# Cross attention over the memory on one Trainium2 core: probabilities divided by GpSimd before their transposes, attention output written already transposed, weight low parts moved to VectorE

## The chip, the cores and the metric

The kernel runs on 1 core of a Trainium2 chip. The metric is the device time of one execution in microseconds (us); the kernel before takes 676.6 us (median of 3 runs, 676.42 to 676.83). TensorE is the matmul engine (PE), VectorE is DVE, ScalarE is ACT, GpSimd is POOL.

## The reference

One layer of a hybrid model over 512 tokens of width 1024: a state-space mixer and block attention, then attention over a memory of 256 rows, then a convolutional feed-forward layer. The change lies in the second of these:

```
def memory_cross_attention(h, mem_n, w_q, w_kv, w_o, qn, kn):
    q = rms_norm((h @ w_q).reshape(bsz, t, X_HEADS, X_HEAD_DIM), qn)
    kv = mem_n @ w_kv
    k = rms_norm(kv[..., :D_X].reshape(bsz, m, X_HEADS, X_HEAD_DIM), kn)
    v = kv[..., D_X:].reshape(bsz, m, X_HEADS, X_HEAD_DIM)
    s = jnp.einsum('bqhd,bmhd->bhqm', q, k).astype(jnp.float32) * (X_HEAD_DIM ** -0.5)
    prob = jax.nn.softmax(s, axis=-1).astype(v.dtype)
    o = jnp.einsum('bhqm,bmhd->bqhd', prob, v).reshape(bsz, t, D_X)
    return o @ w_o
```

with 4 heads of width 128 (X_HEADS, X_HEAD_DIM), 512 query tokens t and 256 memory rows m. All is float32.

## The kernel before, in words

Tokens are cut into 4 tiles of 128. Each engine has a program of its own, an order written out by hand, and engines meet at semaphores alone. The large products are made of three matmuls each (`mm3`, L517): a float32 operand is split into a high part (made by ACT, `split_hi` L489 for weights, `tile_hi` L1203 for activations) and a low part (the remainder; DVE, `split_lo` L505 and `tile_lo` L1692), and high x high, high x low and low x high are added up in one PSUM bank. Eight PSUM banks are handed out by a table written at L282 to L344: `fill` waits until the bank's former user was drained, `filled` tells the reader, `drained` frees it.

Attention over the memory is a pipeline over 16 heads s = 0..15 (tile t = s // 4, head h = s % 4), L2486 on PE, L1336 on ACT, L1859 on DVE. For each head, in iteration s unless another is given:

- PE, scores (L2462), two heads ahead: 128 queries x 256 memory rows, into bank 3, 4 or 5.
- DVE, the negated row maximum (`row_max` L1852), one head ahead.
- ACT, one head ahead (`x_probabilities` L1322): maximum times the query's norm factor, then exp into one of two slots of `pbuf`, with the row sum into `lsum`. It waits until PE has transposed head s-2 out of that slot.
- PE, two 128x128 transposes of the unnormalised probabilities into bank 6 (`prob_transposes` L2276).
- Evacuation into `ptb` (`xp_evac` L405): ACT for even heads, DVE for odd ones.
- PE, one head later, values (`x_values` L2308): stationary operand is the transposed probabilities, moving operand is V, so queries lie on partitions; four heads fill bank 7.

After the fourth head of a tile, DVE's `normalise` (L1683) multiplies the bank by the reciprocals of the four row sums into `yrow`; PE transposes that tile by four 128x128 transposes (`xo_transposes` L2469), ACT makes the high and DVE the low part (`xo_hi` L1316, `xo_lo` L1826), and PE multiplies by w_o in four pieces (`xo_piece` L2422; each 6 matmuls of 512 columns). Between the heads PE runs other work: pieces of the query projection (`xq_piece`) up to s = 6, then those of the output projection, (0,0) at s = 7 up to (2,0) at s = 15; (2,1) to (3,3) follow after the loop. The weights of w_o are units U_XO + 0..3. Their high parts are made by ACT at s = 5..8 (`XO_AT`), their low parts by POOL (`output_low` L972), which has little else to do here: norm factors (`pow_event` L876). `w_residual` (L1830, DVE) adds a finished half tile to `hres` and frees its bank. `root` (L1438, DVE) sharpens POOL's factor by four small operations, `qx_event` (L1823, DVE) sums the squares of a query tile, `transposed` (L1642, DVE) brings a transposed query tile in.

In DVE's loop every iteration begins with the row maximum; then come, where due, the normalisation, the evacuation of head s-1, the query tile, `qx_event`, `root`, `xo_lo` and `w_residual`.

Of the kernel before, what the change touches and what calls it, by code (L numbers as in the profile page):

```python
# [20 lines left out]
TT = T // 128  # L21
# [6 lines left out]
M = 256  # L28
MT = M // 128
# [76 lines left out]
def layer(nc, A, out):  # L106
# [11 lines left out]
    with ctx:  # L118
# [149 lines left out]
        logit_ready, pv_done = sem("logit_ready"), sem("pv_done")  # L268
        rl_ready, rlrow_ready, ya_ready = sem("rl_ready"), sem("rlrow_ready"), sem("ya_ready")
        yasq_ready, yasum_ready = sem("yasq_ready"), sem("yasum_ready")  # L270
        qr_ready = sem("qr_ready")
        conv_ready, gate_ready = sem("conv_ready"), sem("gate_ready")
        hff_ready, res_ready = sem("hff_ready"), sem("res_ready")
        cube_sq, cube_ready, cube_tanh, half_ready = (sem(n) for n in ("cube_sq", "cube_ready", "cube_tanh", "half_ready"))


        QXT_BANK, XO_BANK, W_BANK = (0, 1, 2, 0), (1, 0, 1, 7), (2, 1, 2, 0, 2, 1, 3, 2)


        uses, fills = {}, [0] * 8  # L280
# [5 lines left out]
        def plan():  # L286
            use(4, "nmix"); use(5, "lam")
            for b in range(4):
                use(b, f"xa{b}")
            for b in range(4):  # L290
                use(4 + b, f"xc{b}")
            use(6, "cr"); use(7, "cm"); use(4, "xb"); use(5, "par"); use(6, "relb")
            for m in range(4):
                use(m, f"u{m}")

            def four(pre):
                for i in range(4):
                    use(6 + i % 2, f"{pre}{i}")
            for p in "qkv":
                for t in range(TT):  # L300
                    use(t, f"{p}{t}")
            for q in range(NQ):
                use(4, f"w1r{q}"); use(5, f"w1i{q}"); use(6, f"ka{q}"); use(7, f"kb{q}")
                use(4, f"vr{q}"); use(5, f"vi{q}")
                if q > 0:
                    four(("qt", "m", "kt")[q - 1])
                use(6, f"ye{q}"); use(7, f"yo{q}")
            for s in range(TT * H):
                use(3 + s % 2, f"sc{s}"); use(5 + s % 2, f"pt{s}")
                if s >= H and s % H == 0:  # L310
                    use(5, f"rl{s // H - 1}")
            for t in range(TT):
                use(7, f"pv{t}")
            use(5, "rl3"); use(6, "sa")
            use(0, "mk0"); use(1, "mk1"); use(2, "mv0"); use(0, "mv1")
            use(1, "z0"); use(2, "z1"); use(0, "z2"); use(1, "z3")
            use(3, "kx0"); use(4, "kx1")
            for t in range(TT):
                for half in range(2):
                    use((2 * t + half) % 3, f"g{t}{half}")  # L320
            for t in range(TT):
                for half in range(2):
                    use((2 * t + half + 2) % 4, f"o{t}{half}")
                    use(4 + (2 * t + half) % 4, f"x2{t}{half}")
            for t in range(TT):
                use(t % 3, f"qx{t}"); use(QXT_BANK[t], f"qxt{t}")

            for s in range(TT * XH):
                use(3 + s % 3, f"xs{s}"); use(6, f"xp{s}")
            for t in range(TT):  # L330
                use(7, f"xpv{t}"); use(XO_BANK[t], f"xo{t}")
                for half in range(2):
                    use(W_BANK[2 * t + half], f"w{t}{half}")
            for t in range(TT):
                for half in range(2):
                    use(4 + (2 * t + half) % 4, f"x3{t}{half}")
            for j in range(2 * FT):
                use(j % 4, f"f{j}")
            for x in range(4):
                for t in range(2):  # L340
                    use(E_BANK[x][t], f"e{x}{t}")
            for x in range(3):
                for t in range(2):
                    use(E_BANK[x][t], f"d{x}{t}")  # L344
# [448 lines left out]
        def _(pool):  # L793
# [175 lines left out]
                link(add(yasq[:, 2, :], yasq[:, 2, :], yasq[:, 3, :]))  # L969
                add(yasum[:, t, :], yasum[:, t, :], yasq[:, 2, :]).then_inc(yasum_ready, 1)  # L970

            def output_low(i):  # L972

                u = U_XO + i
                pool.wait_ge(hi_done, u + 1)
                nc.gpsimd.tensor_tensor(w_unit(u, 1), raw_unit(u), w_unit(u, 0).bitcast(f32), ALU.subtract)\
                    .then_inc(lo_done, 1)

            factor_rows(0)
            link(y_sum(1))  # L980
# [7 lines left out]
            attention_sum(2)  # L988
            factor_rows(3)
            attention_sum(3)  # L990
            for i in range(EVN["ya"], len(EV)):
                pow_event(i)
                if EV[i][0] == "qx2":
                    pool.wait_ge(lo_done, U_XO)
                    for n in range(4):
                        output_low(n)

            def hidden_sums(i):

# [13 lines left out]
        def _(act):  # L1013
# [300 lines left out]
                drained(A_(sqr_x[:, t % 2, :], p[:, :], ACT.Square, scale=rs[:, c:c + 1]), f"qx{t}")  # L1314

            def xo_hi(t):  # L1316
                tile_hi(f"xo{t}", bs[:, 0, :].rearrange("p (a n) -> p a n", a=4)[:, :, t * 128:(t + 1) * 128])

            qx_rows(0)
            qx_rows(1)  # L1320
# [88 lines left out]
        def _(dve):  # L1409
# [270 lines left out]
            dve.wait_ge(far_zero, 1)  # L1680
            dve.wait_ge(bias_in, 16)

            def normalise(bank, l0, heads, width, t):  # L1683

                p = read(dve, bank)
                link(V.reciprocal(rl[:, 0:heads], lsum[:, l0:l0 + heads]))
                drained(tt(yrow[:, t, :].rearrange("p (h n) -> p h n", h=heads),
                           p[:, :].rearrange("p (h n) -> p h n", h=heads),
                           rl[:, 0:heads].unsqueeze(2).to_broadcast([128, heads, width]), ALU.mult), bank)
                after_drain(dve, bank)  # L1690

            def tile_lo(name, hi, lo, last=True):  # L1692

                ins = lo_of(read(dve, name)[:, :].rearrange("p (a n) -> p a n", a=4), hi, lo)
# [130 lines left out]

            def xo_lo(t):  # L1826
                v = [bs[:, i, :].rearrange("p (a n) -> p a n", a=4)[:, :, t * 128:(t + 1) * 128] for i in range(2)]
                tile_lo(f"xo{t}", v[0], v[1])

            def w_residual(t, halves=range(2)):  # L1830
                for half in halves:
# [20 lines left out]
            def row_max(s):  # L1852
# [2 lines left out]
                V.tensor_reduce(nmx[:, 32 + s:33 + s], p[:, 0:M], AX.X, ALU.max, negate=True)\  # L1855
                    .then_inc(logit_ready, 1)

            row_max(0)
            for s in range(TT * XH):  # L1859
                if s + 1 < TT * XH:  # L1860
                    row_max(s + 1)
                if s in (5, 9, 13):
                    t = (s - 5) // 4
                    normalise(f"xpv{t}", 32 + XH * t, XH, XD, t)
                if s >= 2 and s % 2 == 0:
                    xp_evac(dve, V.tensor_copy, s - 1)
                if s in (1, 5, 9):
                    transposed("qxt", qT, "x_qn", XD ** -0.5, [1 + s // 4])
                if s in (4, 8):
                    qx_event(1 + s // 4)  # L1870
                if s in (2, 6, 10):
                    root(f"qx{1 + s // 4}", qr_ready)
                if s in (6, 10, 14):
                    xo_lo((s - 6) // 4)
                if s in (10, 12):
                    w_residual(0, [s // 2 - 5])
                if s == 14:
                    w_residual(1, [0])
                    x3_mean(0)
            xp_evac(dve, V.tensor_copy, TT * XH - 1)  # L1880
            normalise(f"xpv{TT - 1}", 32 + XH * (TT - 1), XH, XD, TT - 1)
            x3_rows(0)
            w_residual(1, [1])
            xo_lo(TT - 1)
            w_residual(2, [0])
            x3_mean(1)
            w_residual(2, [1])
# [110 lines left out]
        def _(pe):  # L1998
# [275 lines left out]
                            filled(last, f"sc{s + b}")  # L2274

            def prob_transposes(pre, sc, s, tiles, ring, last_of_fill=True):  # L2276
                after_drain(pe, f"{sc}{s}")
                p = fill(pe, f"{pre}{s}")
                for a in range(tiles):
                    last = tr(p[:, a * 128:(a + 1) * 128], pbuf[:, s % ring, a * 128:(a + 1) * 128])  # L2280
                if last_of_fill:
                    filled(last, f"{pre}{s}")
# [25 lines left out]
            def x_values(s):  # L2308
                t, h = s // XH, s % XH
                after_drain(pe, f"xp{s}")  # L2310
                p = fill(pe, f"xpv{t}") if h == 0 else pb[uses[f"xpv{t}"][0]]
                for a in range(MT):
                    last = mm(p[:, h * XD:(h + 1) * XD], ptb[:, s % 2, a * 128:(a + 1) * 128],
                              xv[:, a, h * XD:(h + 1) * XD], a == 0, a == MT - 1)
                if h == XH - 1:
                    filled(last, f"xpv{t}")
                else:
                    last.then_inc(pv_done, 1)
# [147 lines left out]
                p = fill(pe, f"xs{s}")  # L2466
                filled(mm(p[:, 0:M], qT[:, h, t * 128:(t + 1) * 128], kxT[:, h, :]), f"xs{s}")

            def xo_transposes(t):  # L2469
                after_drain(pe, f"xpv{t}")  # L2470
                tile_transposes(f"xo{t}", yrow[:, t, :])

            def x3_transposes(t):
                pe.wait_ge(xn_ready, NMK + t + 1)
                h_transposes("x3", t, x3row[:, t % 2, :])
# [10 lines left out]
            for s in range(TT * XH):  # L2486
# [7 lines left out]
                    xq_piece((s + 1) // XH + 2, (s + 1) % XH)  # L2494
                else:
                    if (s + 1) % XH == 0:
                        after_drain(pe, f"xo{(s + 1) // XH - 2}")
                    xo_piece((s + 1) // XH - 2, (s + 1) % XH)
                prob_transposes("xp", "xs", s, MT, 2)
                if s >= 1:  # L2500
                    x_values(s - 1)
                if s in (5, 9, 13):
                    xo_transposes((s - 5) // 4)
            x_values(TT * XH - 1)
            for i in range(1, 4):
                xo_piece(2, i)
                if i == 2:
                    xo_transposes(3)
            x3_transposes(0)
            after_drain(pe, "xo3")  # L2510
            for i in range(4):
                xo_piece(3, i)
                if i == 1:
# [82 lines left out]
```

## Time and profile before

| | |
|---|---|
| median of 3 runs | 676.6 us (676.42 to 676.83) |
| the profiled execution | 676.84 us |
| its span in the profile | 675.0 us |
| PE busy | 664.4 us, 98% |
| DVE busy | 489.7 us, 73% |
| ACT busy | 345.0 us, 51% |
| POOL busy | 178.6 us, 26% |
| loop over the 16 heads | about 269 to 311 us of the span |
| granted TensorE clock | 1.00 in this stretch |

The profiled execution takes 1.8 us more than its span, which lies around it and does not depend on the kernel's middle. In a timeline a row is start, duration, engine, line of the code, operation, output and inputs, and in brackets the idle time of the engine ahead of it with what ended it. Matmuls overlap, so what one costs PE is the distance from its start to the start of the next; on DVE and ACT one instruction starts some 0.08 to 0.1 us before the record of the one ahead ends. A float32 matmul is two instructions, a transpose one.

### The profile page before, as it was taken

Reading aid. Unit: us, or ns where it says so; the run is one execution under the profiler, and the core shown is the slowest. Engines: PE = TensorE matmul, PEld = TensorE weight load, DVE = VectorE, ACT = ScalarE, POOL = GpSimd, SP = SyncE. Lnnn points to the kernel's source line nnn. Section 1 sums busy time; section 2 is a strip of 40 time slices with the busy share of each in tenths; the row PEclk is TensorE's granted clock in tenths of the full one; section 3 lists DMA queues with packets and bytes.
Section 4 is the critical chain, followed back from the end, with each engine's and each line's share of the span. In section 5 each row is a group of like instructions: output and inputs, shape, how many; then the busy total and the mean of one; then the engine's idle time right before and its main releaser. Section 6 shows DMA issues by size and latency. Waiting matters only on the chain.

```text
span 675.0 us, 10889 instructions
## 1 busy us (share of the span) xinstructions
PE 664.4 (98%) x4039; PEld 550.3 (82%) x4039; DVE 489.7 (73%) x807; ACT 345.0 (51%) x602; POOL 178.6 (26%) x184
## 2 busy tenths in 40 slices
PE   7999999999999999999999999999999999999997
PEld 6978877877778788888998888888888888888886
DVE  3999998849765657556877675666566687867967
ACT  4747654676844544664454433333333454554662
POOL 4899997033221101240101111011101121100000
PEclk9999999999999999999999999999999999999999
DMA  8737563577210215030337557555556446654563
GB/s 257 225 82 183 118 186 102 156 223 258 64 63 2 98 59 187 1 124 1 126 125 249 191 186 242 191 183 187 190 191 227 146 183 210 226 186 141 178 197 124
DMA packets 73919, 105.76 MB, mean 157 GB/s; under 512 B 21929, under 2 KB 48852, under 8 KB 72340
## 3 DMA queue, kind: packets, MB, share of 16 engines
q1 hardware_dynamic: 70612, 98.89, 45.3%
q10 hardware_dynamic: 3264, 6.31, 2.9%
q8 instruction: 25, 0.41, 0.2%
q14 instruction: 18, 0.15, 0.1%
HBM read 88.27 MB, written 17.31 MB: 156 GB/s over the span
## 4 chain that ended last, share of the span: by engine, by line
PE 82%; DMA 4%; POOL 4%; ACT 4%; SPq 3%; DVE 2%; issue 1%; DVEq 0%; ACTq 0%; POOLq 0%
PE pb L519 24%; PE pb L521 24%; PE pb L520 23%; PE pb L2000 7%; PE pb L2003 4%; POOL F L802 2%; ACT F L1022 2%; SPq L679 2%; DMA raw<-in_w_in 1%; DMA F<-F 1%; DMA raw<-in_x_wkv 1%; DVE F L1420 1%; DMA F<-scr_y 1%; SPq L692 0%; ACT xs L1022 0%
## 5 line engine op out<-in xcount | busy, mean ns | idle before, releaser
L519 PE MATMUL pb<-xs,wring 128*128 128x512 f32 (+1 forms) x448 | 165.3, 369 | 0.1
L521 PE MATMUL pb<-xs,wring 128*128 128x512 f32 (+1 forms) x448 | 164.2, 366 | 0.0
L520 PE MATMUL pb<-xs,wring 128*128 128x512 f32 (+1 forms) x448 | 164.1, 366 | 0.0
L1426 DVE SCALAR_TENSOR_TENSOR F<-pb,ccol,F 128x511 f32<-128x511 f32 x88 | 65.9, 749 | 71.7 <-ACT F L1022 69.9
L509 DVE TENSOR_TENSOR wring<-raw,wring 128x1024 fp32r<-128x1024 f32 x73 | 97.5, 1338 | 6.1 <-ACT wring L498 5.9
L519 PE MATMUL pb<-wring,xs 128*128 128x512 f32 x240 | 99.1, 413 | 0.5 <-DVE wring L512 0.3
L519 PEld LDWEIGHTS pb<-xs,wring 128*128 128x128 f32 x448 | 84.5, 189 | 14.5 <-issue 0.6
L521 PEld LDWEIGHTS pb<-xs,wring 128*128 128x128 f32 x448 | 84.5, 189 | 13.7
L520 PEld LDWEIGHTS pb<-xs,wring 128*128 128x128 f32 x448 | 84.5, 189 | 13.5
L521 PE MATMUL pb<-wring,xs 128*128 128x512 f32 x240 | 94.0, 392 | 0.0
L520 PE MATMUL pb<-wring,xs 128*128 128x512 f32 x240 | 93.7, 390 | 0.0
L1022 ACT ACTIVATE F<-pb,ccol 128x512 f32<-128x512 f32 x44 | 34.3, 779 | 115.3 <-PE pb L521 115.1
L498 ACT ACTIVATE wring<-raw 128x1024 fp32r<-128x1024 f32 x78 | 81.8, 1054 | 15.1 <-DMA raw<-in_w_in 6.5
L519 PE MATMUL pb<-wring,bs 128*128 128x512 f32 x170 | 68.6, 404 | 0.6 <-DVE wring L1420 0.5
L828 POOL TENSOR_TENSOR F<-F 128x256 f32<-128x256 f32 x27 | 21.8, 809 | 172.8 <-DVE F L1420 171.4
L521 PE MATMUL pb<-wring,bs 128*128 128x512 f32 x170 | 66.3, 390 | 0.0
L520 PE MATMUL pb<-wring,bs 128*128 128x512 f32 x170 | 66.2, 390 | 0.0
L1022 ACT ACTIVATE F<-pb 16x128 f32<-16x128 f32 (+5 forms) x84 | 31.1, 383 | 56.9 <-PE pb L2003 49.0
L2000 PE MATMUL pb<-F 128*64 128x64 f32 (+6 forms) x1056 | 58.5, 256 | 1.5 <-DVE F L1420 0.7
L2000 PEld LDWEIGHTS pb<-F 128*64 128x64 f32 (+4 forms) x1056 | 45.2, 143 | 14.0 <-issue 10.6
L519 PEld LDWEIGHTS pb<-wring,xs 128*128 128x128 f32 x240 | 45.1, 188 | 12.0 <-issue 1.6
L521 PEld LDWEIGHTS pb<-wring,xs 128*128 128x128 f32 x240 | 45.1, 188 | 10.0
(160 smaller groups left out, 989.6 us busy)
## 6 DMA issues: line engine op xcount, KB each, us to landing
raw<-in_ffn_w_up SPq DMA_DIRECT2D x22, 1024.0 KB, 5.2
F<-in_ffn_w_down SPq DMA_DIRECT2D x11, 1024.0 KB, 5.0
scr_w<-F SPq DMA_DIRECT2D x11, 1024.0 KB, 3.9
F<-in_x SPq DMA_DIRECT2D x8, 512.0 KB, 5.9
raw<-in_w_in ACTq DMA_DIRECT2D x4, 1024.0 KB, 6.0
raw<-in_w_out SPq DMA_DIRECT2D x4, 1024.0 KB, 4.9
raw<-scr_w SPq DMA_DIRECT2D x8, 512.0 KB, 3.8
raw<-scr_w SPq DMA_DIRECT2D x15, 256.0 KB, 4.7
```

The costliest lines, as they stand in the source:

```text
L498: ins = nc.scalar.activation(w_unit(u, 0), raw_unit(u), ACT.Copy)
L509: ins = nc.vector.tensor_tensor(w_unit(u, 1), raw_unit(u), w_unit(u, 0).bitcast(f32), ALU.subtract)
L519: nc.tensor.matmul(ps, lh, rh, start=first, stop=False)
L520: nc.tensor.matmul(ps, lh, rl_, start=False, stop=False)
L521: return nc.tensor.matmul(ps, ll, rh, start=False, stop=last)
L679: sync.dma_start(toep[d * CG:(d + 1) * CG, :, (L - 1 - d) * CG:], kt[0:CG, :, 0:(d + 1) * CG]).then_inc(t_in[q], 16)
L802: return nc.gpsimd.tensor_tensor(o, a, b, ALU.mult)
L828: return nc.gpsimd.tensor_tensor(o, a, b, ALU.subtract)
L1022: return nc.scalar.activation(o, i, f, **k)
L1426: return V.scalar_tensor_tensor(out=o, in0=a, scalar=s1, in1=b, op0=o1, op1=o2)
L2000: return nc.tensor.matmul(o, l, r, start=start, stop=stop)
L2003: return nc.tensor.transpose(o, i, ident[0:i.shape[0], 0:i.shape[0]])
```

## The change

- The 16 row sums get a reciprocal each on DVE (`inverse_sum`), behind DVE's other work of iteration s-1, and POOL multiplies the 128x256 probabilities of each head in place (`scale_probabilities`). PE's transposes of head s wait for that in place of ACT's exp.
- `x_values` swaps its operands: V is stationary, the transposed probabilities move, so the output has head dimensions on partitions. `normalise` and `xo_transposes` are gone, and `xo_hi` and `xo_lo` read the bank of the values.
- The row maximum is taken two heads ahead on DVE.
- The low parts of the four units of w_o are made on DVE at s = 6..9, in place of POOL.
- PSUM banks are handed out anew, and the last `xo_lo` stands ahead of `w_residual(1, [1])`.

```diff
-        QXT_BANK, XO_BANK, W_BANK = (0, 1, 2, 0), (1, 0, 1, 7), (2, 1, 2, 0, 2, 1, 3, 2)
+        QXT_BANK, XPV_BANK, W_BANK = (0, 1, 2, 7), (7, 1, 7, 1), (2, 0, 2, 0, 2, 3, 0, 2)
...
-            def output_low(i):
-
-                u = U_XO + i
-                pool.wait_ge(hi_done, u + 1)
-                nc.gpsimd.tensor_tensor(w_unit(u, 1), raw_unit(u), w_unit(u, 0).bitcast(f32), ALU.subtract)\
-                    .then_inc(lo_done, 1)
+            def scale_probabilities(s):
+
+                pool.wait_ge(xinv_ready, s + 1)
+                nc.gpsimd.tensor_scalar_mul(pbuf[:, s % 2, 0:M], pbuf[:, s % 2, 0:M], rl[:, s % 4:s % 4 + 1])\
+                    .then_inc(xprob_ready, 1)
...
-            for i in range(EVN["ya"], len(EV)):
+            for i in range(EVN["ya"], EVN["qx2"]):
                 pow_event(i)
-                if EV[i][0] == "qx2":
-                    pool.wait_ge(lo_done, U_XO)
-                    for n in range(4):
-                        output_low(n)
+            for s in range(TT * XH):
+                if s in (6, 10):
+                    pow_event(EVN["qx2"] + s // 10)
+                scale_probabilities(s)
+            for i in range(EVN["x30"], len(EV)):
+                pow_event(i)
...
+            def inverse_sum(s):
+
+                after_drain(dve, f"xs{s}")
+                V.reciprocal(rl[:, s % 4:s % 4 + 1], lsum[:, 32 + s:33 + s]).then_inc(xinv_ready, 1)
+
             row_max(0)
+            row_max(1)
+            inverse_sum(0)
             for s in range(TT * XH):
-                if s + 1 < TT * XH:
-                    row_max(s + 1)
-                if s in (5, 9, 13):
-                    t = (s - 5) // 4
-                    normalise(f"xpv{t}", 32 + XH * t, XH, XD, t)
+                if s + 2 < TT * XH:
+                    row_max(s + 2)
...
                 if s in (6, 10, 14):
                     xo_lo((s - 6) // 4)
+                if s + 1 < TT * XH:
+                    inverse_sum(s + 1)
+                if s - 1 in XO_AT:
+                    split_lo(dve, U_XO + XO_AT.index(s - 1))
                 if s in (10, 12):
                     w_residual(0, [s // 2 - 5])
...
             xp_evac(dve, V.tensor_copy, TT * XH - 1)
-            normalise(f"xpv{TT - 1}", 32 + XH * (TT - 1), XH, XD, TT - 1)
             x3_rows(0)
+            xo_lo(TT - 1)
             w_residual(1, [1])
-            xo_lo(TT - 1)
...
             def prob_transposes(pre, sc, s, tiles, ring, last_of_fill=True):
-                after_drain(pe, f"{sc}{s}")
+                if pre == "xp":
+                    pe.wait_ge(xprob_ready, s + 1)
+                else:
+                    after_drain(pe, f"{sc}{s}")
...
                 for a in range(MT):
-                    last = mm(p[:, h * XD:(h + 1) * XD], ptb[:, s % 2, a * 128:(a + 1) * 128],
-                              xv[:, a, h * XD:(h + 1) * XD], a == 0, a == MT - 1)
+                    last = mm(p[:, h * XD:(h + 1) * XD], xv[:, a, h * XD:(h + 1) * XD],
+                              ptb[:, s % 2, a * 128:(a + 1) * 128], a == 0, a == MT - 1)
...
                 if s >= 1:
                     x_values(s - 1)
-                if s in (5, 9, 13):
-                    xo_transposes((s - 5) // 4)
             x_values(TT * XH - 1)
             for i in range(1, 4):
                 xo_piece(2, i)
-                if i == 2:
-                    xo_transposes(3)
             x3_transposes(0)
-            after_drain(pe, "xo3")
+            after_drain(pe, "xpv3")
```

## Rows read from the trace of the kernel before

**Rows 1.** The page, busy time by engine: busy us, share, instructions
```profile
PE 664.4 (98%) x4039; PEld 550.3 (82%) x4039; DVE 489.7 (73%) x807; ACT 345.0 (51%) x602; POOL 178.6 (26%) x184
```

**Rows 2.** Engines in a window of the span: us, busy (count) by engine, clock, DMA
```profile
262.00:325.00 63.00, 62.73 (x351) 52.81 (x351) 38.09 (x92) 35.88 (x85) 15.12 (x11) 1.00 0.16 57
```

**Rows 3.** Timeline of PE, the start of the loop and iterations 5 to 8
```profile
270.89 0.38 PE L2003 MATMUL pb<-ident,pbuf 128*128 128x128 f32 x2
...
284.43 0.60 PE L2003 MATMUL pb<-ident,F 128*128 128x128 f32 x4
284.86 0.60 PE L2000 MATMUL pb<-F 128*128 128x256 f32 x2
...
287.60 0.58 PE L519 MATMUL pb<-wring,bs 128*128 128x512 f32 x1
...
292.76 0.60 PE L2000 MATMUL pb<-F 128*128 128x256 f32 x2
293.30 0.50 PE L519 MATMUL pb<-wring,bs 128*128 128x512 f32 x1
```

**Rows 4.** Timeline of PE, iterations 10 to 15
```profile
297.93 1.04 PE L2000 MATMUL pb<-F 128*128 128x128 f32 x6
298.69 0.51 PE L519 MATMUL pb<-wring,bs 128*128 128x512 f32 x1
...
305.85 0.60 PE L2003 MATMUL pb<-ident,F 128*128 128x128 f32 x4
306.20 0.47 PE L519 MATMUL pb<-wring,bs 128*128 128x512 f32 x1
...
307.88 0.61 PE L2000 MATMUL pb<-F 128*128 128x128 f32 x4
308.62 0.47 PE L519 MATMUL pb<-wring,bs 128*128 128x512 f32 x1
```

**Rows 5.** Timeline of DVE: reciprocal, evacuation, squares, row maximum
```profile
281.69 0.18 DVE L1686 RECIPROCAL rl<-lsum 128x4 f32<-128x4 f32 x1 [1.32 <-PE pb L2000]
...
289.65 0.42 DVE L412 COPY F<-pb 128x256 f32<-128x256 f32 x1 [1.24 <-PE pb L2003]
290.00 0.68 DVE L1468 TENSOR_REDUCE sq<-F 128x4 f32<-128x512 f32 x1
...
290.78 0.42 DVE L1855 TENSOR_REDUCE nmx<-pb 128x1 f32<-128x256 f32 x1
```

**Rows 6.** Timeline of DVE: root, low part of the output, residual, a weight's low part
```profile
296.58 0.16 DVE L1420 TENSOR_TENSOR rt<-rs 128x4 f32<-128x4 f32 x1 [0.88 <-POOL rs L879]
...
297.26 0.69 DVE L1426 SCALAR_TENSOR_TENSOR bs<-pb,bs 128x512 fp32r<-128x512 f32 x1
297.87 0.68 DVE L1426 SCALAR_TENSOR_TENSOR F<-pb,F 128x512 f32<-128x512 f32 x1
...
320.88 1.22 DVE L509 TENSOR_TENSOR wring<-raw,wring 128x1024 fp32r<-128x1024 f32 x1
```

**Rows 7.** Timeline of ACT: end of the first head's exp
```profile
270.47 0.19 ACT L1022 ACTIVATION_READ_ACCUMULATOR pbuf<-pb,nmx,rs 128x1 f32 x1
```

**Rows 8.** Groups of POOL's instructions by form: count, busy us, mean ns
```profile
L976 POOL TENSOR_TENSOR wring<-raw,wring 128x1024 fp32r<-128x1024 f32 x4 | 9.5, 2380 | 5.0 <-ACT wring L498 5.0
...
L958 POOL COPY F<-rl 128x512 f32<-128x512 f32 x4 | 2.5, 621 | 18.6 <-DVE rl L1711 18.6
...
L828 POOL TENSOR_TENSOR pbuf<-F,pbuf 128x256 f32<-128x256 f32 x2 | 2.1, 1038 | 0.2
...
L831 POOL TENSOR_SCALAR sp<-sp 128x16 f32<-128x16 f32 x3 | 0.6, 205 | 0.3
```

**Rows 9.** Timeline: POOL and DVE at the same time in the stage before
```profile
157.44 1.55 POOL L952 TENSOR_SCALAR F<-F 128x512 f32<-128x512 f32 x1
157.54 1.63 DVE L509 TENSOR_TENSOR wring<-raw,wring 128x1024 fp32r<-128x1024 f32 x1
```

**Rows 10.** Timeline of POOL and of DVE, a small operation beside POOL's low part
```profile
283.66 2.37 POOL L976 TENSOR_TENSOR wring<-raw,wring 128x1024 fp32r<-128x1024 f32 x1 [2.52 <-ACT wring L498]
...
284.59 1.46 DVE L1420 TENSOR_TENSOR rt<-rs 128x4 f32<-128x4 f32 x1
```

More of the change, by code:

```diff
@@ L270, in layer @@
         yasq_ready, yasum_ready = sem("yasq_ready"), sem("yasum_ready")
-        qr_ready = sem("qr_ready")
+        qr_ready, xinv_ready, xprob_ready = sem("qr_ready"), sem("xinv_ready"), sem("xprob_ready")
         conv_ready, gate_ready = sem("conv_ready"), sem("gate_ready")
@@ L325, in plan @@
             for t in range(TT):
-                use(t % 3, f"qx{t}"); use(QXT_BANK[t], f"qxt{t}")
+                use(t % 3, f"qx{t}")
+                if t < TT - 1:
+                    use(QXT_BANK[t], f"qxt{t}")
             for s in range(TT * XH):
@@ L330, in plan @@
             for t in range(TT):
-                use(7, f"xpv{t}"); use(XO_BANK[t], f"xo{t}")
+                if t == 2:
+                    use(QXT_BANK[3], "qxt3")
+                use(XPV_BANK[t], f"xpv{t}")
                 for half in range(2):
@@ L1316, in xo_hi @@
             def xo_hi(t):
-                tile_hi(f"xo{t}", bs[:, 0, :].rearrange("p (a n) -> p a n", a=4)[:, :, t * 128:(t + 1) * 128])
+                tile_hi(f"xpv{t}", bs[:, 0, :].rearrange("p (a n) -> p a n", a=4)[:, :, t * 128:(t + 1) * 128])
             qx_rows(0)
@@ L1681, in _ @@
             dve.wait_ge(bias_in, 16)
[L1683 to L1690, printed above, removed]
             def tile_lo(name, hi, lo, last=True):
@@ L1827, in xo_lo @@
                 v = [bs[:, i, :].rearrange("p (a n) -> p a n", a=4)[:, :, t * 128:(t + 1) * 128] for i in range(2)]
-                tile_lo(f"xo{t}", v[0], v[1])
+                tile_lo(f"xpv{t}", v[0], v[1])
             def w_residual(t, halves=range(2)):
@@ L2467, in x_scores @@
                 filled(mm(p[:, 0:M], qT[:, h, t * 128:(t + 1) * 128], kxT[:, h, :]), f"xs{s}")
-            def xo_transposes(t):
-                after_drain(pe, f"xpv{t}")
-                tile_transposes(f"xo{t}", yrow[:, t, :])
             def x3_transposes(t):
@@ L2496, in _ @@
                     if (s + 1) % XH == 0:
-                        after_drain(pe, f"xo{(s + 1) // XH - 2}")
+                        after_drain(pe, f"xpv{(s + 1) // XH - 2}")
                     xo_piece((s + 1) // XH - 2, (s + 1) % XH)
```

## The prediction

> **What bounds the kernel now.** I began with the page's busy times [rows 1]: PE is busy for 664.4 of 675.0 us. Then I took the stretch that the change touches out of the table of windows [rows 2]: PE is busy for 62.73 of 63 us at full granted clock, DVE for 38, ACT for 36 and POOL for 15. So work taken off DVE, ACT or POOL buys nothing by itself. Only two things move the end: PE instructions that vanish, and waits of PE that vanish or appear. The third view, the timeline of PE [rows 3, 4], shows which waits there are, and the fourth, DVE's timeline [rows 5, 6], how late DVE is in each iteration. Averages mislead here: DVE is busy 60% of the stretch, yet its in-order queue decides when PE may start a piece.
>
> **What PE loses.** The four groups of four output transposes go. From the start of such a group to the next instruction it is 284.86 - 284.43 = 0.43 us in front of scores [rows 3] and 306.20 - 305.85 = 0.35 us in front of a piece [rows 4]. Two are of either kind: 0.43 + 0.43 + 0.35 + 0.35 = 1.56 us. The swap of operands in the values keeps count and shape (two float32 products of 128 columns by 128x128 per head): 0, since weight loads run beside matmuls for both; no row shows the swapped form, and I bound it at 0.05 us a head either way. `normalise` leaves DVE; PE never waited on it visibly.
>
> **What is added on the path to a transpose.** exp, then reciprocal on DVE, then the multiplication on POOL, then the transposes. The reciprocal has 0.18 us [rows 5]. No row shows a scaling of 128x256 on POOL. Nearest from below: a one-input copy of 128x512 takes 0.62 and a 128x16 scaling 0.205 [rows 8], which gives a line of 0.84 ns a column and 0.40 us for 256 columns; half the copy, 0.31, is the lower end. From above, a two-input operation on the same buffer and size takes 1.04 [rows 8]. I take 0.40, as the operation has one input like the copy. Each hand-over between engines costs about 0.05 to 0.1.
>
> At the first head nothing covers this. Its exp ends at 270.47 + 0.19 = 270.66 [rows 7], and PE transposes at 270.89 [rows 3]. Now: 270.66 + 0.05 + 0.18 + 0.13 + 0.40 + 0.08 = 271.50, so **+0.6 us**. For all later heads exp starts once PE has transposed the head two before, that is two iterations ahead: an iteration without query transposes is 2.74 - 0.25 = 2.49 us, so 4.98. ACT is busy for 36 us over 16 heads in the stretch [rows 2], 2.2 us a head with everything that could stand ahead of an exp, and the 0.8 us above follow: 3.0 of 4.98, so **0**. That cover is gone only if POOL needs over 2 us a head.
>
> **What DVE makes late.** This is the main term. With the maximum two heads ahead, DVE's iteration s begins with scores s+2, and these are PE's first work of iteration s itself. Everything due in that DVE iteration stands behind them. Measured from the start of those scores: filled at 0.60 [rows 3], hand-over 0.05, maximum 0.34 (0.42 less the 0.08 by which the next record overlaps), evacuation 0.35, `qx_event` 0.78 [rows 5], `root` 0.68, `xo_lo` 0.61, residual or weight low part to its end 0.68 or 1.22 [rows 6], reciprocal 0.10 of spacing, hand-over to PE 0.04. PE itself needs 287.60 - 284.86 = 2.74 us from those scores to the next piece [rows 3].
>
> - Piece (0,0), s = 7, needs the low part that DVE makes at the end of its iteration 6: 0.60 + 0.05 + 0.34 + 0.35 + 0.68 + 0.61 + 0.10 + 1.22 + 0.04 = 3.99 against 2.74. PE waits **1.25 us**, before 0. POOL had it ready.
> - Piece (0,2), s = 9: behind `qx_event` 3.48 against 2.74 + 0.43 for the query transposes = 3.17. Wait 0.31. Before, 293.30 - 292.76 = 0.54 where 0.25 is due, 0.29 of waiting for POOL [rows 3]. Net **0**.
> - Piece (1,0), s = 11, needs the bank that the first residual frees, in DVE's iteration 10: 0.60 + 0.05 + 0.34 + 0.35 + 0.68 + 0.61 + 0.10 + 0.68 + 0.04 = 3.45 against 2.74, wait 0.71. Before, 298.69 - 297.93 = 0.76 where 0.70 is due, 0.06 [rows 4]. Net **+0.65**. So the transposes saved just ahead of it are handed back.
> - Piece (2,0), s = 15, hangs on a chain from the transposes of head 13: exp 15, `xo_hi`, `xo_lo`, residual. It gated already: values end at 307.88 + 0.44 = 308.32, the piece starts at 308.62 [rows 4], 0.30 of wait. The chain stays and gains a reciprocal of 0.10. PE gets there 0.35 earlier and waits that long more: **+0.45** against the 0.35 saved.
>
> **What meets on the shared side.** The GpSimd scaling of head 7 starts with the low part of unit 0 on DVE, as both follow the same reciprocal. Rows show such a meeting: the DVE low part took 1.63 beside POOL's scaling of 512 columns, which took 1.55 [rows 9], against 1.22 alone [rows 6] and 0.62 for a copy of that size. That is 0.41 on DVE, and for 256 columns half: 0.2 for each of the two low parts that gate, **+0.4**. Harder cases exist: a 0.16 us operation stood 1.46 us beside POOL's 2.37 us one, until that ended [rows 10]. The Trainium skill (GPSIMD Reference, Key points) says that GpSimd shares its SBUF interfaces with VectorE and meets instructions with two SBUF inputs; a weight's low part is one. Taken as full blocking for the length of the scaling this gives the third rival.
>
> **Sum.** +0.6 + 1.25 + 0 + 0.65 + 0.45 + 0.4 - 1.56 = +1.8 us. The profiled execution took 676.84 (span 675.0), 0.24 above the median of 676.6; on the median I forecast **678.4**. The phase after it is bound by PE too, so the shift passes through. Ends of the unknown terms: scaling 0.31, no meeting and hand-overs 0.3 lower give +1.0; scaling 1.04 and meetings of full size give +2.9. A difference below 0.2% (1.35 us) can't be told from none here.
>
> **Rivals.**
>
> - *DVE keeps up* (faster). Mechanism: the low part of unit 0 reaches PE within the 2.74 us, since DVE's hand-overs overlap more than its rows say. It decides when that part lies below about 2.9. Then the waits before (0,0) and (1,0) and the meetings go too, and what is left is +0.6 + 0.45 - 1.56 - 0.29 - 0.06 - 0.2 = -1.1 to -1.6: 675.3. For it: PE is the bound and loses instructions for certain. Against: 3.99 is a sum of eight rows, each measured here. Chance 0.10.
> - *Half of it* (no change). Only one of the two long waits comes, or the first head's +0.6 is hidden by the slack of iteration 0. That takes 0.65 to 1.25 off the sum: 677.3. Chance 0.25.
> - *POOL and DVE block each other wholly.* A scaling stands until the low part is through, and DVE's small two-input operations stand behind a scaling: 0.4 for each of the two gating parts in place of 0.2, and some 0.3 in `root` ahead of (0,0) and (1,0). +1.8 + 0.4 + 0.6 = +2.8: 679.4. For it: the 1.46 us row; against: in the order of the queues `root` mostly runs when POOL is idle. Chance 0.13.
> - *The scaling is slow* (over 2 us a head, as POOL's 2.38 us for 1024 columns of two inputs [rows 8]). Then it gates transposes throughout: 2 us at the first head plus some tenths in each of 15, above 681. Chance 0.03, as the 512 column copy speaks against it.
>
> The forecast itself has 0.49.
>
> **How the numbers follow.** Slower by over 0.2%: nearly all of the forecast (0.45 of 0.49) and the last two, 0.61. Within: the second rival and the rest of the forecast, 0.29. Faster: 0.10. The forecast's own range is +1.0 to +2.9, 677.6 to 679.5; to hold 8 in 10 it reaches down through the second rival and up through the third: 676.3 to 680.0.
>
> **What would show it.** In the changed kernel's timeline of PE: the first probability transposes 0.6 us after their former place; a gap of about 1.2 us ahead of the first output piece at s = 7, named as a wait for DVE's low part; gaps of 0.3, 0.7 and 0.7 us ahead of (0,2), (1,0) and (2,0), the last two ended by a residual; no output transposes. POOL's scaling near 0.4 us, longer beside a low part. I am wrong if PE shows no gap at s = 7, or if the sum of PE's waits in the stretch stays below 1.5 us.

## The result, and the profile after

The changed kernel takes 679.99 us (median of 5 runs, 679.21 to 681.73) against 676.42 (675.95 to 676.83): a ratio of 1.0056, 95% interval 1.0040 to 1.0072. It is slower, as forecast, but by 3.6 us where 1.8 were forecast. The page of the kernel after, busy times by engine:

```profile
span 678.2 us, 10872 instructions
PE 663.7 (98%) x4023; PEld 549.1 (81%) x4023; DVE 488.4 (72%) x819; ACT 345.2 (51%) x602; POOL 186.9 (28%) x196
```

PE has lost 16 instructions and 0.7 us of work, yet the span is 3.2 us longer: the difference lies in waits. The same window as [rows 2], and the one behind it:

```profile
262.00:325.00 63.00, 59.96 (x323) 49.37 (x321) 37.57 (x102) 35.10 (x85) 23.43 (x23) 1.00 0.16 55
325.00:350.00 25.00, 23.22 (x195) 23.25 (x196) 16.63 (x28) 10.26 (x14) 1.46 (x1) 1.00 0.27 86
```

PE was busy 62.73 of 63 us here before; now it is 59.96, and 1.8 us are missing in the next 25, at full clock. PE's timeline shows where; these rows answer to [rows 3, 4] (lines are 3 to 4 higher in this kernel):

```profile
271.68 0.44 PE L2006 MATMUL pb<-ident,pbuf 128*128 128x128 f32 x2 [0.90 <-POOL pbuf L979]
...
287.31 1.04 PE L2003 MATMUL pb<-F 128*128 128x128 f32 x6
289.24 0.47 PE L523 MATMUL pb<-wring,bs 128*128 128x512 f32 x1 [0.88 <-issue]
...
294.27 0.60 PE L2003 MATMUL pb<-F 128*128 128x256 f32 x2
294.78 0.50 PE L523 MATMUL pb<-wring,bs 128*128 128x512 f32 x1
...
298.98 1.04 PE L2003 MATMUL pb<-F 128*128 128x128 f32 x6
300.41 0.47 PE L523 MATMUL pb<-wring,bs 128*128 128x512 f32 x1 [0.38 <-DVE F L1431]
...
309.12 0.61 PE L2003 MATMUL pb<-F 128*128 128x128 f32 x4
310.34 0.47 PE L523 MATMUL pb<-wring,bs 128*128 128x512 f32 x1 [0.60 <-DVE F L1431]
...
326.78 0.36 PE L523 MATMUL pb<-xs,wring 128*128 128x256 f32 x1 [1.92 <-DVE F L1431]
```

The first five are the places of the forecast. A wait is the distance between two starts less what it is without one; the idle time in brackets is often shorter than that. Ahead of (0,0): 289.24 - 287.31 - 0.70 = 1.23 us. Ahead of (0,2): 294.78 - 294.27 - 0.25 = 0.26. Ahead of (1,0): 1.43 - 0.70 = 0.73. Ahead of (2,0): 1.22 - 0.44 = 0.78. The sixth is new to me: 1.92 us ahead of the first feed-forward matmul, which is no part of the attention.

Single executions differ by up to 1.6 us ahead of this stage (first scores at 266.68 to 268.29 in the profiles); PE waits there, at about 11 us, between 0 and 2.4 us for the input x. So below I measure the **stretch** from PE's first scores to its first feed-forward matmul, whose two starts stand in the timeline. Behind it all profiles but one agree to 0.15 us (351.3 to 351.4 to the end of the span).

| kernel | first scores | first feed-forward matmul | stretch |
|---|---|---|---|
| before | 268.21 | 323.65 | 55.44 |
| after | 267.94 | 326.78 | 58.84 |

58.84 - 55.44 = 3.40 us, the whole difference (the part ahead is 0.27 shorter, the part behind 0.07 longer). Up to the first of the two last groups of eight transposes in the output projection (L2006 at 317.45 after, L2003 at 316.18 before) 49.51 against 47.97 have passed, +1.54; the other +1.86 is the sixth wait.

### The profile page after: what moved, and what is told of

The parts are those of the page before. It is cut to its first block, busy times and chain, and to the rows that moved or that the text cites. A ratio compares the mean times of both kernels' runs of the same rounds, so it can differ in the third digit from the quotient of the medians.

```text
span 678.2 us, 10872 instructions
## 1 busy us (share of the span) xinstructions
PE 663.7 (98%) x4023; PEld 549.1 (81%) x4023; DVE 488.4 (72%) x819; ACT 345.2 (51%) x602; POOL 186.9 (28%) x196
## 4 chain that ended last, share of the span: by engine, by line
PE 82%; POOL 4%; ACT 4%; DVE 3%; DMA 3%; SPq 2%; issue 2%; DVEq 0%; ACTq 0%; POOLq 0%
PE pb L523 24%; PE pb L525 24%; PE pb L524 23%; PE pb L2003 7%; PE pb L2006 4%; POOL F L806 2%; DMA raw<-in_w_in 2%; ACT F L1027 1%; DMA raw<-in_x_wkv 1%; DVE F L1425 1%; SPq L683 1%; DMA F<-scr_y 1%; DVE wring L513 1%; ACT xs L1027 1%; SPq L696 1%
## 5 line engine op out<-in xcount | busy, mean ns | idle before, releaser
L1431 DVE SCALAR_TENSOR_TENSOR F<-pb,ccol,F 128x511 f32<-128x511 f32 x88 | 65.9, 749 | 71.6 <-ACT F L1027 69.8
L513 DVE TENSOR_TENSOR wring<-raw,wring 128x1024 fp32r<-128x1024 f32 x77 | 102.0, 1327 | 7.2 <-ACT wring L502 7.1
L2003 PE MATMUL pb<-F 128*64 128x64 f32 (+6 forms) x1056 | 58.2, 256 | 1.5 <-DVE F L1425 0.7
L2003 PEld LDWEIGHTS pb<-F 128*64 128x64 f32 (+4 forms) x1056 | 45.1, 143 | 13.9 <-issue 11.0
```

Source lines behind the costliest of these rows:

```text
L513: ins = nc.vector.tensor_tensor(w_unit(u, 1), raw_unit(u), w_unit(u, 0).bitcast(f32), ALU.subtract)
L1431: return V.scalar_tensor_tensor(out=o, in0=a, scalar=s1, in1=b, op0=o1, op1=o2)
L2003: return nc.tensor.matmul(o, l, r, start=start, stop=stop)
```

## The experiments

All are built on the changed kernel unless said otherwise. Ratios are to the kernel before.

### 1. One bank number

The new table gives bank 0 to w30, the first half tile of the last quarter of the output projection. Bank 0 is also f0's, the first feed-forward unit's, so PE may not start it until DVE's `w_residual(3)` has emptied the bank. Before, w30 had bank 3 and w31 bank 2, which f3 and f2 take later.

```diff
-        QXT_BANK, XPV_BANK, W_BANK = (0, 1, 2, 7), (7, 1, 7, 1), (2, 0, 2, 0, 2, 3, 0, 2)
+        QXT_BANK, XPV_BANK, W_BANK = (0, 1, 2, 7), (7, 1, 7, 1), (2, 0, 2, 0, 2, 3, 1, 2)
```

> The changed kernel with one bank number altered: the half tile w30 of the output projection goes to bank 1 in place of bank 0, so the first feed-forward unit (f0, bank 0) no longer waits for the residual that empties it. Theory (the new table of banks costs the time that the forecast missed): the 1.92 us wait of PE ahead of the feed-forward phase goes, 1.9 us faster than the changed kernel, ratio to before about 1.0024. Rival (DVE and ACT arrive late at that place because the stage before ran differently, and the bank is only where it shows): a wait of 1 us or more stays in front of f0 or f1, and the ratio stays near 1.005.

676.96 us, ratio 1.0013 (1.0003 to 1.0022); stretch 266.79 to 323.56 = 56.77, 2.07 less than after. DVE's timeline, first after, then with bank 1, the residual (L1431, two in one row) and what was ahead of it:

```profile
324.81 1.22 DVE L513 TENSOR_TENSOR wring<-raw,wring 128x1024 fp32r<-128x1024 f32 x1 [0.79 <-ACT wring L502]
325.95 1.28 DVE L1431 SCALAR_TENSOR_TENSOR F<-pb,F 128x512 f32<-128x512 f32 x2
```

```profile
323.68 1.22 DVE L513 TENSOR_TENSOR wring<-raw,wring 128x1024 fp32r<-128x1024 f32 x1 [0.80 <-ACT wring L502]
324.82 1.28 DVE L1431 SCALAR_TENSOR_TENSOR F<-pb,F 128x512 f32<-128x512 f32 x2
```

DVE is exactly as late in both, 1.13 us earlier in absolute time for the second since that whole profile is (first scores 266.79 against 267.94). Only PE no longer waits. The theory holds and the rival falls. The two profiled executions lie 3.3 us apart (679.99 and 676.68): 2.07 of it is this stretch, 1.15 lies ahead of it, where the two kernels are alike. The stretch is therefore the better measure of the edit than the two times.

### 2. That number alone, in the kernel before

```diff
-        QXT_BANK, XO_BANK, W_BANK = (0, 1, 2, 0), (1, 0, 1, 7), (2, 1, 2, 0, 2, 1, 3, 2)
+        QXT_BANK, XO_BANK, W_BANK = (0, 1, 2, 0), (1, 0, 1, 7), (2, 1, 2, 0, 2, 1, 0, 2)
```

> The kernel before with only that bank number of the change: w30 in bank 0 in place of bank 3, all else as before. Theory: a wait of some 1.9 us appears ahead of the feed-forward phase, ratio to before about 1.003. Rival: without the rest of the change the residual is in time, no wait over 0.5 us, ratio 1.000.

680.2 us, ratio 1.0058 (1.0041 to 1.0075), more than either theory. The stretch is 268.29 to 325.69 = 57.40, +1.96 as expected. The rest lies behind it, 352.91 in place of 351.35 to the end of the span. PE's wait, and the windows that follow:

```profile
325.69 0.36 PE L519 MATMUL pb<-xs,wring 128*128 128x256 f32 x1 [1.93 <-DVE F L1426]
```

```profile
326.00:328.00 2.00, 2.00 (x14) 2.00 (x13) 1.86 (x6) 1.82 (x3) 0.00 (x0) 0.64 0.92 291
328.00:330.00 2.00, 2.00 (x11) 2.00 (x10) 2.00 (x4) 0.28 (x1) 0.62 (x1) 0.50 0.70 241
330.00:332.00 2.00, 2.00 (x18) 2.00 (x18) 1.42 (x6) 0.00 (x0) 0.84 (x1) 1.00 0.13 33
```

The granted clock (third number from the right) falls to its lower level, 1.2 GHz, for some 3 us, beginning within a microsecond of the end of the 1.9 us wait, and costs 352.91 - 351.35 = 1.56 us. In all four runs of this kernel the mean clock is 0.994 to 0.997, and no run of the kernel before beside them is below 0.997.

### 3. The row maximum one head ahead again

On top of experiment 1: `row_max(s + 1)` in place of `row_max(s + 2)`, and no `row_max(1)` ahead of the loop.

> As a1_bank, and the row maximum is one head ahead again, in its old place at the head of DVE's iteration. Theory (waiting for scores s+2 at the head of iteration s makes DVE late for the output pieces): the wait ahead of piece (0,0) falls from 1.2 to about 0.6 us, since the chain then goes over exp of head 7, the high and the low part of the output and the weight's low part, and the one ahead of (1,0) from 0.7 to about 0.1; about 1.2 us faster than a1_bank. Rival (the work itself, a low part of 1.2 us more in the iteration, makes DVE late, wherever the maximum stands): both waits stay within 0.2 us.

677.93 us, ratio 1.0022 (1.0012 to 1.0032), an interval that overlaps that of experiment 1. The stretch is 267.54 to 324.37 = 56.83, within 0.1 us of the 56.77 with the bank alone. The part up to piece (0,0) is 0.65 shorter (20.66 against 21.31), as the theory had it, but the same amount is lost behind it: some 0.3 us more ahead of each of (0,1), (0,3) and (1,0). DVE's timeline ahead of (1,0):

```profile
297.75 0.17 DVE L1425 TENSOR_TENSOR rs<-rs,rt 128x4 f32<-128x4 f32 x1
298.61 0.69 DVE L1431 SCALAR_TENSOR_TENSOR bs<-pb,bs 128x512 fp32r<-128x512 f32 x1 [0.69 <-ACT bs L1027]
```

DVE stands 0.69 us for ACT's high part, which stands behind exp of head 11, which stands behind a maximum that DVE gave late, behind its own low part (L513 at 295.37). (0,1) and (0,3) start right at the end of DVE's low parts, which stand behind a reciprocal that waited for exp. So the maximum a head sooner saves at the later pieces what it costs at (0,0). The theory was right at (0,0) and wrong at (1,0), and with it the 1.2 us of gain.

### 4. The low parts on GpSimd again

On top of experiment 1: `output_low(s - 6)` behind the scaling of heads 6 to 9, and no `split_lo` in DVE's loop.

> As a1_bank, and the four low parts of the output weights are on GpSimd again, one behind the scaling of each of heads 6 to 9. Theory: the wait of 1.2 us ahead of (0,0) goes, but GpSimd then needs 2.37 + 0.93 = 3.3 us a head against PE's 2.5, so waits of about 0.8 us appear ahead of (0,1), (0,2) and (0,3); in sum 0.5 to 1 us slower than a1_bank. Rival (VectorE's low parts are the whole loss): 1.2 us faster than a1_bank.

679.44 us, ratio 1.0052 (1.0036 to 1.0069); the stretch is 267.11 to 326.05 = 58.94, 2.17 more than experiment 1. Worse than I had it, since the wait ahead of (0,0) does not go. GpSimd and DVE:

```profile
284.73 2.39 POOL L980 TENSOR_TENSOR wring<-raw,wring 128x1024 fp32r<-128x1024 f32 x1
```

```profile
285.75 1.39 DVE L1436 TENSOR_TENSOR rt<-rs 128x4 f32<-128x4 f32 x1
```

```profile
288.40 0.50 PE L523 MATMUL pb<-wring,bs 128*128 128x512 f32 x1 [0.88 <-DVE bs L1442]
```

The first operation of `root`, 0.15 us otherwise, stands until GpSimd's low part ends at 287.12, and holds up the output's low part that (0,0) needs: the meeting of [rows 10]. Against experiment 1, PE waits 1.0 us more ahead of (0,1) and 0.8 ahead of (0,3), both ended by GpSimd's low parts, but only 0.1 ahead of (0,2), and 0.4 more ahead of the transposes of head 10. In this kernel these parts are better off on VectorE; the rival that they are the whole loss falls.

### 5. High and low parts one head earlier

```diff
-XO_AT = [5, 6, 7, 8]
+XO_AT = [4, 5, 6, 7]
```

> As a1_bank, and the four output weight units are split one head earlier, high parts at s = 4..7 and low parts at s = 5..8. Nothing is taken off VectorE. Theory (the length of DVE's iteration 6 makes PE wait, not the amount of DVE work): the wait ahead of piece (0,0) goes from 1.2 us to under 0.2, since that iteration then ends with the low part of the output, and the one ahead of (0,2) goes too; from the first scores to the feed-forward phase 1.2 to 1.4 us less than a1_bank. Rival (VectorE has too much work in the stretch): the wait turns up ahead of another piece, less than 0.4 us gained.

676.98 us, ratio 1.0004 (0.9995 to 1.0014); the stretch is 266.68 to 322.59 = 55.91, 0.86 less than experiment 1. The wait ahead of (0,0) is gone (the piece starts 20.06 us behind the first scores in place of 21.31), and so is the one ahead of (0,2). A smaller one came, ahead of the transposes of head 7:

```profile
288.71 0.44 PE L2006 MATMUL pb<-ident,pbuf 128*128 128x128 f32 x2 [0.23 <-POOL pbuf L979]
```

From piece (0,0) to these transposes it is 1.97 us where 1.57 are due (289.17 - 287.60 in the kernel before), so this wait costs 0.4. VectorE does the same work as before this edit, so its amount was not the cause of the wait ahead of (0,0); where it stood was. I had 1.2 to 1.4 and forgot that the scaling of head 7 now meets another low part, at the iteration's end; the 0.86 lies between my two theories.

### 6. Three residuals one iteration earlier

On top of experiment 5:

```diff
-                if s in (10, 12):
-                    w_residual(0, [s // 2 - 5])
+                if s in (9, 11):
+                    w_residual(0, [(s - 9) // 2])
+                if s == 13:
+                    w_residual(1, [0])
                 if s == 14:
-                    w_residual(1, [0])
                     x3_mean(0)
```

> As e1_low_one_earlier, and the first three residuals stand one DVE iteration earlier (s = 9, 11, 13 for 10, 12, 14). Theory: the waits ahead of (1,0), 0.7 us, and (2,0), 0.8 us, are waits for a bank that those residuals empty; the first goes to under 0.1, the second to under 0.2, where the low part of the output is next in line; 1.1 to 1.4 us less than e1_low_one_earlier. Rival: root and the low part of the output are what is late there (they are wanted one piece later), the wait moves to (0,3) or (1,1) and under 0.5 us is gained.

675.05 us, ratio 0.9985 (0.9975 to 0.9995). The stretch is 266.85 to 321.46 = 54.61, 1.30 less than experiment 5, in the expected range, and no wait of PE for a residual is left in the loop. Those two waits were for banks. This is the first version that is faster than the kernel before.

### 7. Head 0 divided on VectorE

On top of experiment 6:

```diff
             inverse_sum(0)
+            dve.wait_ge(xinv_ready, 1)
+            V.tensor_scalar_mul(pbuf[:, 0, 0:M], pbuf[:, 0, 0:M], rl[:, 0:1]).then_inc(xprob_ready, 1)
```

with GpSimd's loop from head 1 on, behind a wait for VectorE's product.

> As f1_residual_earlier, and the probabilities of head 0 alone are divided on VectorE. Theory (0.93 us of GpSimd stand open at the first head and nowhere else): the wait ahead of the first probability transposes falls from 1.05 to 0.3 to 0.5 us, the rest of the stage is unchanged: 0.6 us less than f1_residual_earlier. Rival (the hand-overs between engines are the cost): under 0.2 us.

675.21 us, ratio 0.9975 (0.9966 to 0.9985), an interval that overlaps that of experiment 6, so the gain over it is read from the stretch. This is 267.45 to 321.42 = 53.97: 0.64 less than experiment 6, as expected, and 1.47 less than the kernel before. The first transposes come 3.11 us behind the first scores in place of 3.75, which is the whole 0.64. DVE's and PE's rows:

```profile
270.15 0.35 DVE L1864 TENSOR_SCALAR pbuf<-pbuf,rl 128x256 f32<-128x256 f32 x1
```

```profile
270.56 0.44 PE L2010 MATMUL pb<-ident,pbuf 128*128 128x128 f32 x2 [0.26 <-DVE pbuf L1864]
```

VectorE needs 0.35 us for what GpSimd does in 0.93, 0.58 less of the 0.64: the duration was the cost, as the theory says, and not the hand-overs. **This version beats both kernels.** What it gains over the kernel before are the output transposes that the change was to save, 1.75 us by the rows of the next section, and some small waits, less 0.4 us each at the transposes of heads 0 and 7.

### 8. Every head scaled twice

On top of experiment 1, GpSimd multiplies by 1 once more behind each scaling.

> As a1_bank, and GpSimd multiplies every head's probabilities a second time, by 1. Theory (GpSimd is covered at all heads but the first): 0.93 us more at the first transposes, plus at most 0.5 where a stretched operation beside a low part of VectorE comes too late. Rival (GpSimd's scaling is on the path at every head): 0.5 us or more at each of several later heads, 4 us or more in sum.

681.3 us (2 runs), ratio 1.0068 (1.0048 to 1.0088); the stretch is 267.50 to 328.43 = 60.93, 4.16 more. Neither theory gave this; the rival's 4 us is met in number, but not by its mechanism alone. The first transposes come 1.00 later (4.75 against 3.75 behind the first scores), as expected for GpSimd's second 0.92. PE's wait there, and the windows behind it:

```profile
272.25 0.44 PE L2007 MATMUL pb<-ident,pbuf 128*128 128x128 f32 x2 [1.91 <-POOL pbuf L980]
```

```profile
272.20:274.00 1.80, 1.75 (x10) 1.59 (x11) 0.40 (x2) 1.22 (x4) 1.71 (x2) 0.87 0.00 0
274.00:276.00 2.00, 2.00 (x6) 1.41 (x6) 0.75 (x3) 0.00 (x0) 1.18 (x3) 0.50 0.00 0
276.00:278.00 2.00, 2.00 (x12) 1.87 (x11) 0.33 (x1) 0.95 (x3) 0.78 (x1) 0.77 0.00 0
```

Again the granted clock falls to 0.5 soon after a wait of 1.9 us: from there to (0,0) 1.55 us are lost (23.86 - 21.31 - 1.00). The other 1.6 are waits for GpSimd at the transposes of heads 7, 9 and 10, 0.7, 0.3 and 1.0 us, less the wait ahead of (1,0), which they take up. At twice the load, then, the cover of later heads is gone at heads 7 to 10, where `pow_event` and the low parts stand beside it; at the load of the change it holds but for the 0.4 us at head 7 of experiments 5 to 7.

## Why the prediction was right or wrong

The direction, the mechanism inside the loop (DVE's queue, not its load) and the places there were right; the size was half of what was measured, since one wait outside the loop was missed.

| term | forecast, us | measured, us |
|---|---|---|
| output transposes gone | -1.56 | -1.75 |
| first probability transposes | +0.6 | +1.06 (3.74 against 2.68 behind the first scores) |
| wait ahead of (0,0) | +1.25 | +1.23 |
| (0,2) | 0 | -0.03 |
| (1,0) | +0.65 | +0.67 |
| (2,0) | +0.45 | +0.48 |
| VectorE's low parts beside the scaling | +0.4 | 0 |
| rest (pieces a little shorter behind a wait) | not seen | -0.1 |
| w30 in bank 0 | not seen | +1.86 |
| sum | +1.8 | +3.4 |

**The step that failed is an omission.** I wrote "The phase after it is bound by PE too, so the shift passes through". The diff changes a table of banks, and I followed it for the pieces inside the loop alone. The number for w30 makes the first feed-forward unit wait for DVE's last residuals, 1.86 us in the stretch. Experiment 1 takes it away, experiment 2 puts it into the kernel before. All of it could have been read ahead of time: the entry, the use of bank 0 by f0, and DVE's order, in which `w_residual(3)` stands behind two low parts.

Without that entry the rest of the sum is 3.40 - 1.86 = +1.54 against the +1.8 of the forecast. That it comes so near is in part luck: the two waits of DVE's queue were right, but the first head cost 0.46 more, the meetings 0.4 less, and the transposes saved 0.2 more than forecast, and these cancel.

**The transposes were undercounted.** I took the distance from a group of output transposes to the next start, 0.35 us in front of a piece. That leaves out what the start of the next piece overlaps with the group. From the probability transposes of head 13 to those of head 14, before and then after:

```profile
305.18 0.38 PE L2003 MATMUL pb<-ident,pbuf 128*128 128x128 f32 x2
...
307.66 0.38 PE L2003 MATMUL pb<-ident,pbuf 128*128 128x128 f32 x2
```

```profile
306.85 0.38 PE L2006 MATMUL pb<-ident,pbuf 128*128 128x128 f32 x2
...
308.91 0.38 PE L2006 MATMUL pb<-ident,pbuf 128*128 128x128 f32 x2
```

2.06 against 2.48, 0.42 less. The other three groups give 0.45, 0.42 and 0.46 in the same way, 1.75 in all.

**The scaling was mis-sized.** "I take 0.40, as the operation has one input like the copy": alone it takes 0.93. The row for it stood in my own rows, the same kind of operation (by a constant) of 512 columns with 1.55 us [rows 9]. I read that as 0.6 stretched by a meeting. GpSimd's timeline of the kernel after:

```profile
270.69 1.84 POOL L979 TENSOR_SCALAR pbuf<-pbuf,rl 128x256 f32<-128x256 f32 x2 [0.64 <-DVE rl L1857]
...
288.11 3.35 POOL L979 TENSOR_SCALAR pbuf<-pbuf,rl 128x256 f32<-128x256 f32 x2 [2.51 <-DVE rl L1857]
...
293.70 1.82 POOL L979 TENSOR_SCALAR pbuf<-pbuf,rl 128x256 f32<-128x256 f32 x1 [2.23 <-DVE rl L1857]
```

Two undisturbed ones take 1.84, 0.92 each. It cost 0.46 more at the first head, the only one that is not covered in this kernel. Experiment 7 measures the same exposure from the other side.

**The meeting went the other way.** I added 0.2 us to each of two low parts. DVE's, started ahead of the scaling, kept its length:

```profile
287.94 1.20 DVE L513 TENSOR_TENSOR wring<-raw,wring 128x1024 fp32r<-128x1024 f32 x1
```

while GpSimd's operation, started 0.17 us behind it, took about 1.8 in place of 0.93. That is covered, except for the 0.4 us at head 7 in experiments 5 to 7. The Trainium skill (GPSIMD Engine Reference, Key points) says that GpSimd contends with VectorE instructions that have two SBUF inputs. The low part is one, and this trace agrees, with the 1.8 us for 0.93.

Here the operation that started later paid, as in experiment 4, where GpSimd's low part began first and DVE stood. But it does not always stand until the other ends. In [rows 9] DVE's low part starts 0.10 us behind GpSimd's scaling and ends at 159.17, 0.18 us behind the scaling's end at 158.99; had it stood, it would have ended 1.2 us behind. In experiment 4 a small DVE operation of 0.15 us met a scaling in the same way:

```profile
299.24 0.93 POOL L986 TENSOR_SCALAR pbuf<-pbuf,rl 128x256 f32<-128x256 f32 x1
```

```profile
299.28 0.45 DVE L1436 TENSOR_TENSOR rt<-rs 128x4 f32<-128x4 f32 x1 [0.66 <-POOL rs L883]
```

It took 0.3 us longer and ended 0.44 us before the scaling did. The 0.2 us of the forecast belong to this order; in the kernel after, the low part starts first.

Of the rivals, *DVE keeps up* fell, since (0,0) waits 1.23 us, and *half of it*, since both long waits came and the first head's cost too. *The scaling is slow* fell: it takes 0.93 us, and 1.8 beside a low part. *POOL and DVE block each other wholly* gave 679.4, nearer to the time than the forecast, and the first half of its mechanism came: a scaling stood until the low part was through. But that cost nothing, since it was covered; the 0.4 us that it added for each low part did not come, as those kept their length. That its number is near is luck.

## What to carry to other kernels

When a diff renumbers buffers, follow each changed number to its next user, also behind the stage that is changed: a single entry cost more than the change was to save. On an in-order engine the position of a step in its iteration decides, not the engine's load; count from the input that the iteration waits for to the output that somebody needs. Price an operation by the row of the same operation, even at another size and in company, rather than by a cheaper kind of the same size.

## What the runs showed of the hardware that was not expected

- A GpSimd multiplication by a per-partition factor takes 0.93 us for 128x256 float32, VectorE 0.35. GpSimd's 128x512 copy takes 0.62 [rows 8], and its 128x512 scaling by a constant 1.55 [rows 9], so here its one-input operations are not alike.
- Where GpSimd met a VectorE instruction with two SBUF inputs, the one that started later paid in the rows shown. GpSimd's scaling behind DVE's low part stood until that was through (1.8 us for 0.93, the low part 1.20), and DVE's 0.15 us operation behind GpSimd's low part stood too (1.39 us, experiment 4). Behind a GpSimd scaling, DVE was only slowed: a low part by 0.41 us [rows 9], a small operation by 0.3 us (experiment 4).
- In the profiles of experiments 2 and 8 a wait of PE of 1.9 us was followed, within some 1.3 us of its end, by some 3 us at the lower clock level, which cost 1.56 and 1.55 us more. Behind the wait of 1.92 us in the profiled execution of the changed kernel the clock stayed at 1.00, but two of its five executions have a mean clock of 0.997, which is what the one fall gives in experiment 8; the second execution of that kernel has 1.000. So the same kernel can show it in one execution and not in the next. What decides was not tried.
